# Modulation vector of a transformer block: one-column products turned into 256-column products, with the input loads reordered

## What is computed

```python
mod = jnp.einsum('bd,de->be', jax.nn.silu(c), w_ada[l]) + b_ada[l]      # 1024 -> 6*1024, one row
sh1, sc1, g1, sh2, sc2, g2 = [m[:, None, :] for m in jnp.split(mod, 6, axis=-1)]
h = _rms(x, norm1_g[l]) * (1.0 + sc1) + sh1
proj = h @ w_in[l]
...                                                                   # MLA and differential attention
x = x + g1 * (jnp.concatenate([o_mla, o_diff], axis=-1) @ w_o[l])
h2 = _rms(x, norm2_g[l]) * (1.0 + sc2) + sh2
x = x + g2 * _hmoe(h2, ...)
```

## Time and profile before

| | us |
|---|---|
| median of 3 runs (2578.99 to 2584.34) | 2579.84 |
| the profiled execution's own time | 2581.77 |
| its span, first to last instruction | 2580.0 |
| TensorE busy | 2459.5 (95% of the span) |
| VectorE busy | 1611.4 (62%) |
| ScalarE busy | 1211.9 (47%) |
| mean granted clock of TensorE | 0.942 |

### The profile page before, as it was taken

How to read it: one execution, slowest core, us unless ns; L and a number is a source line. 1 busy time by engine, 2 the same in 40 slices (tenths; PEclk the granted TensorE clock), 3 DMA queues, 4 the chain that set the end, 5 groups by cost and what they waited for, 6 DMA issues and landing times.

```text
span 2580.0 us, 38764 instructions
## 1 busy us (share of the span) xinstructions
PE 2459.5 (95%) x16674; PEld 2250.8 (87%) x16674; DVE 1611.4 (62%) x2099; ACT 1211.9 (47%) x1507; POOL 0.2 (0%) x4
## 2 busy tenths in 40 slices
PE   8999989999989899999989899899899999998997
PEld 8898978888889778989869899799689999788997
DVE  6763389999797557444554665596566444545763
ACT  1421357777554353434664444353443434754442
POOL 0000000000000000000000000000000000000000
PEclk7875689999999999999999999899999999989999
DMA  6432249999644324434324354254233433233552
GB/s 250 158 137 98 104 167 372 375 372 370 267 180 165 113 99 144 150 117 146 115 82 147 131 180 163 115 180 164 97 116 131 149 145 131 99 111 135 183 184 92
DMA packets 62332, 427.90 MB, mean 166 GB/s; under 512 B 7632, under 2 KB 10064, under 8 KB 11600
## 3 DMA queue, kind: packets, MB, share of 16 engines
q1 hardware_dynamic: 62160, 425.41, 45.0%
HBM read 424.33 MB, written 1.05 MB: 165 GB/s over the span
## 4 chain that ended last, share of the span: by engine, by line
PE 86%; DVE 5%; ACT 5%; issue 2%; DMA 0%; SPq 0%; DVEq 0%; ACTq 0%
PE banks L1786 54%; PE banks L1804 9%; PE quad L1804 4%; PE single L1520 4%; PE quad L1520 1%; ACT area_y_rounded L661 1%; PE single L574 1%; PE quad L480 1%; PE quad L521 1%; PE single L384 1%; PE quad L379 1%; PE quad L505 1%; DVE slot_rounded L993 1%; PE quad L550 1%; PE banks L1520 1%
## 5 line engine op out<-in xcount | busy, mean ns | idle before, releaser
L1786 PE MATMUL banks<-spare_rounded,slot_rounded 128*128 128x272 f32 (+1 forms) x1920 | 551.3, 287 | 0.0
L1786 PE MATMUL banks<-area_x_rounded,slot_rounded 128*128 128x272 f32 (+1 forms) x1568 | 446.0, 284 | 0.0
L1786 PE MATMUL banks<-spare_rounded,area_y_rounded 128*128 128x272 f32 (+1 forms) x1376 | 401.0, 291 | 13.9 <-DVE hn_rounded L982 13.9
L993 DVE TENSOR_TENSOR slot_rounded<-slot,area_y_rounded 128x2048 fp32r<-128x2048 f32 x118 | 269.9, 2290 | 217.8 <-ACT area_y_rounded L661 217.8
L1786 PE MATMUL banks<-hn_rounded,area_y_rounded 128*128 128x272 f32 (+1 forms) x1376 | 394.7, 287 | 0.0
L1786 PEld LDWEIGHTS banks<-spare_rounded,slot_rounded 128*128 128x128 f32 x1920 | 365.4, 190 | 0.0
L1786 PEld LDWEIGHTS banks<-area_x_rounded,slot_rounded 128*128 128x128 f32 x1568 | 296.3, 189 | 0.0
L1786 PEld LDWEIGHTS banks<-spare_rounded,area_y_rounded 128*128 128x128 f32 x1376 | 261.7, 190 | 21.7 <-DVE hn_rounded L982 14.7
L1786 PEld LDWEIGHTS banks<-hn_rounded,area_y_rounded 128*128 128x128 f32 x1376 | 261.2, 190 | 0.1
L661 ACT ACTIVATE area_y_rounded<-slot 128x2048 fp32r<-128x2048 f32 x118 | 223.9, 1906 | 43.4 <-PE banks L1786 43.4
L993 DVE TENSOR_TENSOR slot_rounded<-slot,area_x_rounded 128x2048 fp32r<-128x2048 f32 x52 | 119.2, 2292 | 132.1 <-ACT area_x_rounded L661 131.9
(11 more groups left out here) (543 smaller groups left out, 6044.4 us busy)
## 6 DMA issues: line engine op xcount, KB each, us to landing
slot<-in_units_second SPq DMA_DIRECT2D x236, 1024.0 KB, 4.8
slot<-in_units_moe SPq DMA_DIRECT2D x100, 1024.0 KB, 5.2
slot<-in_units_first SPq DMA_DIRECT2D x32, 1024.0 KB, 4.8
spare<-in_units_moe SPq DMA_DIRECT2D x20, 1024.0 KB, 5.6
spare<-in_units_first SPq DMA_DIRECT2D x6, 1024.0 KB, 4.9
slot<-in_units_second SPq DMA_DIRECT2D x8, 768.0 KB, 4.1
const_sb<-in_const SPq DMA_DIRECT2D x1, 1384.0 KB, 19.9
slot<-in_units_first SPq DMA_DIRECT2D x2, 576.0 KB, 3.8
```

What stands on the lines that cost most here:

```text
L993: tt(m.slots_low[slot][:, :], m.slots[slot][:, :], m.mixer_high[n].bitcast(F32), ALU.subtract).then_inc(s.mix_low.sem, 1)
L1786: ins = nc.tensor.matmul(out, weights[w], x[a], start=start and i == 0, stop=stop and i == 2, **kw)
```

## The change

`ada_rows(u)` takes the place of `ada_columns(u)`. Now the moving operand is the weights, 256 columns at a time, and the stationary operand is a column of `silu_c` repeated over 128 columns (a stride of 0): 8 products per unit instead of 16. Each gives 128 equal rows of 256 values. Channel 128*t + p of the result is needed on partition p, which is the diagonal of each 128x128 piece. Two units fill a PSUM bank [128, 512]; VectorE multiplies it by the identity (`diagonal`), and sums along the rows, which leaves one column for each of 4 pieces. In the opening this is done for the two units of each pair of tiles (one multiplication, two sums of two pieces); later `read_ada(u)` does it for units u and u + 1 (one multiplication, one sum of four pieces), once ahead of the heads' queries and keys, six times within the items (`ADA_PAIR_BEHIND`) and once behind them. A new semaphore `ada_read` makes TensorE wait before it overwrites the bank of the late units, whose two halves are now used in turn.

Three further edits: SP loads the first ada unit ahead of x and the constants (a semaphore `loaded_early` of their own), the identity goes from the late constants to the early ones (66 KB more), and the sum of the squares of x is done after four units instead of two.

```diff
-    for u in range(SLOTS):
+    load(0)
+    for to, of in m.early_loads:
+        sp.dma_start(to, of).then_inc(m.loaded_early.sem, 16)
+    for u in range(1, SLOTS):
         load(u)
...
-    def ada_columns(u):
+    def ada_rows(u):
         w = weights(first.ada[u])
-        for c in range(2):
-            out = m.ada_column(2 * u + c)
-            for k in range(KT):
-                ins = nc.tensor.matmul(out, w[:, k * UNIT_COLS + 128 * c:k * UNIT_COLS + 128 * c + 128], m.silu_c[:, k:k + 1],
-                                       start=(k == 0), stop=(k == KT - 1))
+        if u >= 10 and u % 2 == 0:
+            pe.wait_ge(s.ada_read.sem, (u - 10) // 2 + 1)
+        for k in range(KT):
+            ins = nc.tensor.matmul(m.ada_part(u), m.silu_c[:, k:k + 1].to_broadcast([128, 128]), w[:, k * UNIT_COLS:(k + 1) * UNIT_COLS],
+                                   start=(k == 0), stop=(k == KT - 1))
         tick(ins, s.gemm_first)
...
     for n, u in enumerate(ADA_EARLY):
-        ada_columns(u)
-        if n == 1:
+        ada_rows(u)
+        if n == 3:
             pe.wait_ge(s.x_squared.sem, 1)
...
+    def diagonal(bank, out, signal):
+        tick(tt(out, bank.rearrange("p (a b) -> p a b", b=128), m.ident.unsqueeze(1).to_broadcast([128, 4, 128]), ALU.mult), signal)
+        settle()
+    def read_ada(u):
+        v.wait_ge(s.gemm_first.sem, index["ada", u + 1] + 1)
+        diagonal(m.single[:, :], m.diagonal_late, s.ada_read)
+        tick(red(m.mod[:, 2 * u:2 * u + 4], m.diagonal_late, AX_X, ALU.add), s.dve1_step)
...
         v.wait_ge(s.gemm_first.sem, 2 * pair + 2)
+        diagonal(m.ada_bank(pair), m.diagonal_early, s.dve1_step)
+        tick(red(m.mod[:, at:at + 2], m.diagonal_early[:, 0:2, :], AX_X, ALU.add), s.dve1_step)
+        link(red(m.mod[:, KT + at:KT + at + 2], m.diagonal_early[:, 2:4, :], AX_X, ALU.add))
         tick(modulation(at, 2), s.dve1_step)
...
         normalise(i)
+        if i in ADA_PAIR_BEHIND:
+            read_ada(ADA_PAIR_BEHIND[i])
         if i < 7:
             bias_steps(1)
...
-    v.wait_ge(s.gemm_first.sem, index["ada", ADA_UNITS - 1] + 1)
+    read_ada(ADA_UNITS - 2)
...
-            for to, of in ((m.par1, par_first), (m.pos_int, positions), (m.x, x), (const_sb[:, 0:CONST_EARLY], const[:, 0:CONST_EARLY])):
+            for to, of in ((m.par1, par_first), (m.pos_int, positions)):
```

More of the change, by code:

```diff
@@ L207 @@
                 ("lag", PACKED), ("cos", T), ("sin", T)]
-CONST_EARLY = 16 + 384 + 4
+CONST_EARLY = 16 + 384 + 4 + 128
 CONST_AT, CONST = {}, 0
@@ L1407 @@
 ADA_EARLY = [0, 4, 1, 5, 2, 6, 3, 7]
-ADA_AT = 128
+ADA_PAIR_BEHIND = {1: 10, 3: 12, 5: 14, 7: 16, 11: 18, 15: 20}
 W_IN = 9
@@ L1527, in more_ada @@
         for _ in range(n):
-            ada_columns(rest.pop(0))
+            ada_rows(rest.pop(0))
     pe.wait_ge(s.lambda_products.sem, 1)
@@ L2007, in first_scalar @@
     c0 = PAR1_AT["c"][0]
-    act.wait_ge(m.loaded.sem, 16 * 4)
+    act.wait_ge(m.loaded.sem, 16 * 2)
     tick(f(m.silu_c[:, :], m.par1[:, c0:c0 + KT], ACT.Tanh, scale=0.5), s.c_tanh)
+    act.wait_ge(m.loaded_early.sem, 16 * 2)
     tick(f(m.sq1, m.x, ACT.Square), s.x_squared)
@@ L2211, in first_vector @@
     tick(nc.vector.memset(m.upad[:, :, 0:CONV_K - 1], 0.0), s.constants_set)
-    v.wait_ge(m.loaded.sem, 16 * 4)
+    v.wait_ge(m.loaded.sem, 16 * 2)
     for i in range(2):
@@ L2221, in first_vector @@
     link(copy(m.pos[:, :], m.pos_int[:, :]))
+    v.wait_ge(m.loaded_early.sem, 16 * 2)
     for b in range(2):
@@ L2266, in modulation @@
     def modulation(at, n):
-        return tt(m.mod[:, at:at + n], m.ada_column(at, n), p1("b_ada", at, n), ALU.add)
+        return tt(m.mod[:, at:at + n], m.mod[:, at:at + n], p1("b_ada", at, n), ALU.add)
+    def diagonal(bank, out, signal):
[5 more added lines that the diff above has]
+        tick(red(m.mod[:, 2 * u:2 * u + 4], m.diagonal_late, AX_X, ALU.add), s.dve1_step)
     def weights_low(n):
@@ L2366, in first_vector @@
     bias_steps(1)
+    read_ada(8)
     for pair in range(4):
@@ L2547, in first_signals @@
     s.c_tanh = Signal(sem("first_c_tanh"))
+    s.ada_read = Signal(sem("first_ada_read"))
     s.lambda_products = Signal(sem("first_lambda_products"))
@@ L2768, in program @@
         m.root1 = a.cut(SEQ)
+        m.diagonal_early, m.diagonal_late = (work[:, at:at + 512].rearrange("p (a b) -> p a b", b=128) for at in (0, 2048))
         a.at = 2560
@@ L2795, in program @@
         m.single = ctx.enter_context(nc.psum_tensor("single", [128, 512], F32))
[L2796 to L2802, removed]
+        m.ada_bank = lambda pair: m.quad[:, 512 * pair:512 * pair + 512] if pair < 3 else m.gemm[2]
+        m.ada_part = lambda u: (m.ada_bank(u % 4)[:, 256 * (u // 4):256 * (u // 4) + 256] if u < 8 else m.single[:, 256 * (u % 2):256 * (u % 2) + 256])
         m.gather_bank = lambda n: (m.gemm + [m.quad[:, 512 * i:512 * i + 512] for i in range(4)])[n % GATHER_BANKS]
@@ L2889, in program @@
         m.gather_read = gather_read
-        m.loaded, m.loaded_late, stored = Signal(sem("loaded")), Signal(sem("loaded_late")), sem("stored")
+        m.loaded, m.loaded_early, m.loaded_late, stored = Signal(sem("loaded")), Signal(sem("loaded_early")), Signal(sem("loaded_late")), sem("stored")
+        m.early_loads = ((m.x, x), (const_sb[:, 0:CONST_EARLY], const[:, 0:CONST_EARLY]))
         m.late_loads = ((const_sb[:, CONST_EARLY:], const[:, CONST_EARLY:]), (m.par_all[:, :, :], par_second), (m.h[:, :, 0:META], meta))
@@ L2911, in _ @@
         def _(pe):
-            pe.wait_ge(m.loaded.sem, 16 * 4)
+            pe.wait_ge(m.loaded.sem, 16 * 2)
             pe.wait_ge(s.constants_set.sem, 1)
```

## The result

The changed kernel takes 2517.3 us (median of 4 runs, 2515.9 to 2519.4), against 2581.0 us for the kernel before on the same chip. The ratio is 0.9753, 95% interval 0.9736 to 0.9770. The forecast was 2515 us, range 2503 to 2540. The profiled execution took 2515.9 us with a span of 2514.1: 65.9 us less span than before, where the sum said 66.

What follows compares the result with a forecast made beforehand. TensorE, largely one-column products at half clock, was taken to bound attention and the opening. Terms 10.5 + 2.2 + 0.7 + 30.5 + 18.4 + 1.8 + 2 = 66 us off 2579.84 gave 2514, stated as 2515; range 2503 to 2540.

Steps and rivals of the forecast that it cites:

- What a unit costs: Ada unit on TensorE: 6.8 us at half clock, 3.4 at full; the change gives nothing by itself.
- The clock: TensorE: full clock from about 5 us after the first unit starts, about 13 us, and through attention.
- the third rival: Clock falls back in attention: units stay 6.8 us, items 10.4; only opening and units 8 and 9 gain; 2567 us; chance 0.07.
- the fourth: Rival: clock doesn't rise at all, wide products at half clock throughout; +13, 2593 us; chance 0.03.
- Weight loads that don't hide: Rival: wide products' weight loads run before them, not beside; a unit takes 5.1 us; +34, 2549 us; chance 0.03.
- The opening: Start to w_in: becomes VectorE's, w_in starts at 64.1 instead of 74.72 us; -10.5.
- The middle: From w_in start to unit 8 (74.72 to 145.78): nothing changes, 71 us carried over.
- Items: Attention, items 0 to 7 (162.56 to 240.21): 77.65 us becomes 47.1; -30.5.
- The ring of two items: Attention's repeating chain through TensorE and VectorE, from a pair's second unit: two items in 11.9 us, 5.95 each.
- Maps: Maps and last units (240.21 to 285.72): 5.8, 6.2, 6.4, 5.3, 3.4 = 27.1 us; -18.4.
- Behind: Behind attention: unit 23, 24 w_o products and VectorE's last read -1.8; next 48 products -2.
- Rival of VectorE's rings: Rings through VectorE cost more: items 7.5 us instead of 5.95, map pairs as much; 17 less gained, 2532 us; chance 0.11.

Runs made afterwards that it cites:

- one-column control: Kernel with weights stationary and vector column repeated 128 times (2505.5 us), given one moving column instead of 128: 2581.3 us, ratio 0.9989.
- series of moving columns: Kernel with weights stationary and vector column repeated 128 times (2505.5 us), with fewer moving columns: one 2581.3 us, 32 2569.7, 64 2524.2.
- late-units kernel: Changed kernel with the 16 late ada units back in one-column form, without VectorE's eight reads, opening as changed: 2574.5 us, ratio 0.9971.

## Why the prediction was right, point by point

- *What a unit costs.* The prediction had it that a unit costs TensorE the same at the same clock and that the change gives it nothing by itself. Right, and shown at 1.00: 3.47 us wide, 3.57 with the weights stationary and 128 columns moving, 3.47 with one column in the few units that still had that clock (one at 289.98 in the one-column control). At 0.50 one column takes 6.6 to 6.9, and the first 12 wide records, ahead of 13.32, took 0.41 us each, which makes 6.6 a unit.
- *The clock.* Full clock was forecast from about 13 us; the trace has it at 13.32, 4.9 us after the first wide product. It was 1.00 through attention, so both the fall back there (the third rival) and the kernel whose clock never rises (the fourth) are out. That the clock goes by the profile's busy share, which the third rival named, is refuted by the series of moving columns: PE was busy 115.84 of 115.84 us at 0.51 with one column and 57.99 of 58.34 at 1.00 with 64.
- *Weight loads that don't hide.* Refuted by 3.47 us a unit, where that rival had 5.1.
- *The opening*: -9.2, forecast -10.5. The first unit landed at 8.3, not 7.7, and so the four units ended at 24.9, not 24.0; the constants landed at 11.7, not 11.0; and a pair took 8.24, not 8.1. The order of events, and VectorE as its bound, were as written.
- *The middle*: +1.0, forecast 0. TensorE's clock rose 5.85 us after w_in started, against 4.1 before (74.72 to 78.85); 1.7 us more at half clock cost 0.9. That isn't owed to the 23 us of idling ahead of it: the late-units kernel idles there as long and has 4.8, and the kernel before, with 5 us of idling, lies near the low end of the 4 to 6 us that the twelve traces show. It is the spread of single executions.
- *Items*: -32.1, forecast -30.5. The ring of two items was 11.89 as worked out. The first two intervals from unit to unit, 4.44 and 5.43 us, were shorter than the 5.4 and 5.95 in the sum and make up the 1.6: in the first TensorE has no mix yet, and in the second no wait behind a read. VectorE's read cost 1.4 as estimated (0.70 and 0.69, start to start 1.33).
- *Maps*: -18.4, as forecast, but by luck, since the parts were not right. From unit to unit it was 6.1, 6.1, 5.2, 6.1 and 3.6, where I had 5.8, 6.2, 6.4, 5.3 and 3.4: the low half of w_o delayed the fourth pair (TensorE waited 1.44 us) and not the third.
- *Behind*: -5.4, forecast -3.8. This is the term that was mis-sized. Half of the 1.6 us it left out altogether: the last mix, ahead of w_o, took 1.49 us at the lower clock and 0.66 now. The turns and VectorE's last read together cost 0.1 more than the turns alone before (2.71 us against 2.59), where the sum had 0.7. The 48 products of w_o took 6.17 instead of 8.42, 0.25 more than the 2 forecast. Unit 23 and the 24 products ahead of it gave 2.4 as forecast, to 0.1.
- *Rival of VectorE's rings*: it was there in small. TensorE waited 0.5 to 0.8 us for each normalisation behind a read in the MLA items, where 0.8 was counted; taking the diagonals out altogether gave 7.4 us up to the last w_o result, 5.5 of them in the opening.
- *The sum.* It was right to 0.1 us of span by luck: the terms were off by up to 1.6 us (opening, items, behind), the rest by 1.5, and these errors cancelled. What wasn't luck is the mechanism: the clock in attention, and VectorE as the bound of the opening.

## What to carry to other kernels

The matrix-vector product of this kernel cost TensorE 3.5 us a unit at full clock in each form, with one, 64 or 128 columns moving or with the weights moving; what differed was the clock beside it. Where a row shows TensorE busy at a granted clock of 0.50, look at what its products are before counting them: here repeating a one-column operand over 128 columns by a stride of 0 cost 0.1 us a unit at the same clock (3.57 against 3.47), and with the clock that came with it the unit took half as long. And prefer the form whose result lies where it is read: the diagonal was the only new work in this change, 1.4 us of VectorE for each pair of units, and it wasn't needed.

## What the runs showed of the hardware

- With one-column products, 32 records in 6.6 us, the clock was 0.51 in attention although PE was busy for 115.84 of 115.84 us and PEld for 106.36; with 32 columns moving it was the same (0.52), with 64 and with 128 it was 1.00 there but for one drop with 64.
- Rising and holding were not the same: 27.5 us of products with 64 moving columns and nothing else didn't raise the clock in the opening; it rose only with the 256-column squares, at 38.7, and then four more units of 64 columns alone, from 40.5 to 54.9, had it throughout. With 128 columns it rose at 14.0, 6 us after their start.
- The clock that the windows show ahead of the first recorded change (1.00) isn't a measurement: the records there have the pace of half clock, such as 128 records in 27.54 us above and 0.41 us for each of the first 12 of the changed kernel.
- An operand with a stride of 0 cost little or nothing more: as the stationary one 3.47 us for 16 records, as the squares with ordinary operands (3.47); as the moving one 3.57 for 32 records, against 3.47 for 32 with one ordinary column at the same clock.
